# Between two transformer blocks on one core: the low passes of the first projection go ahead of the mean of squares, and half of the third weight slab goes ahead of the gates and decays

## The reference

```python
x = x + rmsnorm(f, norm_mlp_post[l])              # end of the first block
# second block
h = rmsnorm_2(x, norm_mix[layer])                 # x * rsqrt(mean(x*x) + eps) * gain
proj = h @ w_in[layer]
q_nsa, kv_nsa, g_nsa, q_gla, k_gla, v_gla, lr_gla, r_gla, g_merge = split_in_proj(proj)
gates_a = jax.nn.sigmoid(g_nsa)
log_a = jax.nn.log_sigmoid(lr_gla @ gla_gate_w2[layer] + gla_gate_b[layer]) / GLA_GATE_TAU
```

## Time and profile before

| | us |
|---|---|
| median of 3 runs | 1430.52 |
| lowest and highest | 1429.3 and 1430.56 |
| profiled execution, its time | 1429.37 |
| profiled execution, its span | 1427.3 |
| TensorE busy in the span | 1411.2 (99%) |
| VectorE busy in the span | 798.6 (56%) |
| ScalarE busy in the span | 538.3 (38%) |

### The profile page before, as it was taken

How to read it: one execution, slowest core, us unless ns; L and a number is a source line. 1 busy time by engine, 2 the same in 40 slices (tenths; PEclk the granted TensorE clock), 3 DMA queues, 4 the chain that set the end, 5 groups by cost and what they waited for, 6 DMA issues and landing times.

```text
span 1427.3 us, 17634 instructions
## 1 busy us (share of the span) xinstructions
PE 1411.2 (99%) x7303; PEld 1148.1 (80%) x7303; DVE 798.6 (56%) x1126; ACT 538.3 (38%) x768; POOL 173.0 (12%) x145
## 2 busy tenths in 40 slices
PE   7999999999999999999999999999999999999998
PEld 5888788988888888888888776668888888888887
DVE  6998674744234343367494577774545545534533
ACT  6222344643333132255543346662343223212214
POOL 1040013100000000120141612111210000000002
PEclk9999999999999999999999999999999999999999
DMA  6322224112322332323234211112322332232221
GB/s 196 118 89 89 89 89 146 62 59 89 116 90 89 103 104 89 96 89 96 89 81 127 73 60 60 31 31 60 118 89 89 93 113 89 91 116 89 89 89 60
DMA packets 136015, 129.69 MB, mean 91 GB/s; under 512 B 15776, under 2 KB 131424, under 8 KB 135904
## 3 DMA queue, kind: packets, MB, share of 16 engines
q1 hardware_dynamic: 134800, 124.90, 28.1%
q0 software_dynamic: 992, 3.47, 0.8%
q10 hardware_dynamic: 144, 0.20, 0.0%
HBM read 126.06 MB, written 2.10 MB: 90 GB/s over the span
## 4 chain that ended last, share of the span: by engine, by line
PE 95%; ACT 1%; DVE 1%; DMA 1%; issue 1%; POOL 0%; SPq 0%; ACTq 0%
PE gemm L464 75%; PE gemm L572 3%; PE gemm L951 3%; PE misc L972 2%; PE misc L991 1%; PE misc L800 1%; PE gemm L656 1%; PE gemm L603 1%; PE gemm L1032 1%; PE gemm L964 1%; DMA w_raw<-in_w_in 1%; PE misc L964 1%; PE misc L603 1%; PE gemm L1065 1%; PE gemm L677 1%
## 5 line engine op out<-in xcount | busy, mean ns | idle before, releaser
L1668 DVE TENSOR_TENSOR w_lo<-w_raw,w_hi 128x2048 fp32r<-128x2048 f32 (+1 forms) x108 | 245.8, 2276 | 174.7 <-ACT w_hi L1128 174.6
L464 PE MATMUL gemm<-h_hi,w_hi 128*128 128x512 f32 x828 | 325.0, 393 | 0.0
L464 PE MATMUL gemm<-h_hi,w_lo 128*128 128x512 f32 x828 | 322.3, 389 | 0.0
L464 PE MATMUL gemm<-h_lo,w_hi 128*128 128x512 f32 x828 | 322.3, 389 | 0.0
L1128 ACT ACTIVATE w_hi<-w_raw 128x2048 fp32r<-128x2048 f32 (+1 forms) x113 | 213.8, 1892 | 143.9 <-PE gemm L464 139.5
L464 PEld LDWEIGHTS gemm<-h_hi,w_hi 128*128 128x128 f32 x828 | 155.4, 188 | 35.2 <-issue 2.4
L464 PEld LDWEIGHTS gemm<-h_hi,w_lo 128*128 128x128 f32 x828 | 155.5, 188 | 32.4
L464 PEld LDWEIGHTS gemm<-h_lo,w_hi 128*128 128x128 f32 x828 | 155.5, 188 | 32.2 <-issue 0.5
L464 PE MATMUL gemm<-n_hi,w_hi 128*128 128x512 f32 x336 | 130.9, 390 | 0.0
L464 PE MATMUL gemm<-n_lo,w_hi 128*128 128x512 f32 x336 | 130.7, 389 | 0.0
L464 PE MATMUL gemm<-n_hi,w_lo 128*128 128x512 f32 x336 | 130.7, 389 | 0.0
(11 more groups left out here) (463 smaller groups left out, 1967.9 us busy)
## 6 DMA issues: line engine op xcount, KB each, us to landing
w_raw<-in_w_in SPq DMA_DIRECT2D x62, 512.0 KB, 4.6
w_raw<-in_w_down SPq DMA_DIRECT2D x32, 512.0 KB, 4.0
w_raw<-in_w_up SPq DMA_DIRECT2D x28, 512.0 KB, 4.3
w_raw<-in_w_ffn_gate SPq DMA_DIRECT2D x22, 512.0 KB, 4.7
w_raw<-in_w_ffn_up SPq DMA_DIRECT2D x22, 512.0 KB, 4.4
w_raw<-in_w_ffn_down SPq DMA_DIRECT2D x16, 512.0 KB, 4.0
w_raw<-in_w_o SPq DMA_DIRECT2D x8, 512.0 KB, 4.1
w_raw<-in_w_out SPq DMA_DIRECT2D x8, 512.0 KB, 4.0
```

The lines of the kernel that those rows point to most:

```text
L464: mm = nc.tensor.matmul(bank[:], w(s)[:, kt, col0:col0 + P], x(n), start=first, stop=last)
L1668: V.tensor_tensor(part(lo_of(s), s), part(raw_of(s), s), f(part(hi_of(s), s)), SUB).then_inc(S("lo_done"), SLABS_AT[s])
```

## The change

On PE, `first_in` no longer contains the mean nor the spread. Its passes with `u_lo` go tile by tile over the three blocks (one wait for each tile) in place of block by block. Behind it come `mean_rows`, then the first half of the third slab (block m0 + 3) with the spread put in after 5 of its 8 tiles (`SPREAD_AT`), then the gates and decays, then the second half of the third slab (block m0 + 4). On ACT the 8 squares go behind all 8 right half tiles of `u_hi` and behind the high part of the third slab. On DVE the low part of the third slab goes ahead of the reciprocal.

```diff
+    SPREAD_AT = 5
...
             for k in range(KT):
-                pe.wait_ge(S("x1_squared"), KT + k + 1)
-                mm = mean_rows(Y[:, k, :], k == 0, k == KT - 1)
-            mm.then_inc(S("mean_ready"), 1)
-            for n, (s, c0, m) in enumerate(blocks):
-                if n == 1:
-                    spread_rstd(M[2], 4)
-                for k in range(KT):
-                    pe.wait_ge(S("u_lo_ready"), k + 1)
+                pe.wait_ge(S("u_lo_ready"), k + 1)
+                for s, c0, m in blocks:
                     mm = nc.tensor.matmul(G[m % 4][:], hi_of(s)[:, k, c0:c0 + P], ULO[:, k, :], start=False, stop=k == KT - 1)
-                mm.then_inc(S("block_full"), 1)
+                    if k == KT - 1:
+                        mm.then_inc(S("block_full"), 1)
 
         first_in()
+        for k in range(KT):
+            pe.wait_ge(S("x1_squared"), KT + k + 1)
+            mm = mean_rows(Y[:, k, :], k == 0, k == KT - 1)
+        mm.then_inc(S("mean_ready"), 1)
+        pe.wait_ge(S("lo_done"), s0 + 3)
+        gemm(s0 + 2, m0 + 3, range(KT), 0, h(UHI), h(ULO), lambda n: spread_rstd(M[2], 4) if n == SPREAD_AT else None)
         pe.wait_ge(*evac_at(m0))
...
-        slab(s0 + 2, h(UHI), h(ULO))
+        gemm(s0 + 2, m0 + 4, range(KT), P, h(UHI), h(ULO))
         slab(s0 + 3, h(HHI), h(HLO), ready=h_ready(hlo))
...
             nc.scalar.activation(UHI[:, k, SIDE[1]], XT[:, k, SIDE[1]], ACT.Copy, scale=col("norm_mix_2", k)).then_inc(S("u_hi_ready"), 1)
+        split_hi(PH["small"][0] + 2)
+        for k in range(KT):
             nc.scalar.activation(Y[:, k, :], XT[:, k, :], ACT.Square).then_inc(S("x1_squared"), 1)
-        split_hi(PH["small"][0] + 2)
         root_of_rows(5)
...
-        invert_rows(4)
         s0, _, m0, _ = PH["small"]
         split_lo(s0 + 2)
+        invert_rows(4)
```

## The result

| | before | changed |
|---|---|---|
| median of 16 runs, us | 1430.0 | 1436.03 |
| lowest | 1428.7 | 1434.46 |
| profiled execution's span | 1427.3 | 1434.2 |

The changed kernel is slower: ratio 1.0042, 95% interval [1.0029, 1.0054], that is +6.0 us (4.1 to 7.7). The forecast was 1435.2 (1432.9 to 1437.8) and +5.3.

A forecast was written before the change was run, and what follows sets the result against it. TensorE was taken to bound the kernel. Right half -1.6, wait +5.2 and clock +1.7 gave +5.3 us: 1434.7 on the profiled execution, 1435.8 on the median, forecast between at 1435.2, range 1432.9 to 1437.8.

The forecast's parts named there:

- The bound and the room: TensorE bounds; DVE's low part of slab s0 + 3 has 1.82 us of room, and TensorE would wait 5.2 us there.
- The right half: In first_in, u_hi tiles without squares between them come every 0.73 us, at DVE's pace: gain 1.64 us.
- Squares, low passes, mean, spread: Squares and low passes wait for nothing; mean ends 4.1 us late, the copy to rstd comes 5.4 us late.
- The clock: Behind TensorE's stop at slab s0 + 3 the granted clock falls to its lower level: 1.7 us lost, once.
- The next slab: Slab s0 + 4: with the lower clock 5.3 us late without waiting; with full clock waits 0.4, 3.9 late.
- The sum: On the profiled execution, right half, wait and clock: -1.6 + 5.2 + 1.7 = +5.3 us.

The follow-up runs named there:

- run 1: The changed kernel with the spread put in after 2 tiles of block m0 + 3 in place of 5; ratio 1.0019 to the kernel before, median 1433.32 us.
- Run 5: The changed kernel with ACT's squares back between the right half tiles of u_hi; ratio 1.0052 to the kernel before, median 1437.1 us.
- Run 4: The changed kernel with 22 matmuls that nobody reads in front of slab s0 + 3; ratio 1.0034 to the kernel before, median 1435.37 us.
- Run 3: The changed kernel with the high and low parts of slabs s0 + 3 and s0 + 4 moved earlier; ratio 0.9994 to the kernel before, median 1429.99 us.
- Run 3's repetition: The kernel of Run 3 measured once more, unchanged; ratio 1.0 to the kernel before, median 1429.67 against 1429.29 us.
- run 2: The changed kernel with only slab s0 + 3's high and low parts moved earlier; ratio 1.0042 to the kernel before, median 1437.18 us.
- run 9: The kernel before with 8 matmuls that nobody reads behind the third slab; ratio 1.0012 to the kernel before, median 1432.68 us.
- run 10: The kernel before with 16 matmuls that nobody reads behind the third slab; ratio 1.0023 to the kernel before, median 1433.4 us.
- run 6: The kernel before with only ACT's squares moved behind all right half tiles and the third slab's high part; ratio 1.0032, median 1434.08 us.
- run 7: The kernel of Run 3 with 5 wide matmuls between the four groups of narrow ones; ratio 1.0009 to the kernel before, median 1429.93 us.
- run 8: The kernel before with 5 wide matmuls between the four groups of narrow ones; ratio 1.0017 to the kernel before, median 1431.82 us.

## Why the prediction was right, and where it was off

- **The bound and the room.** Right. The room of 1.82 us in front of slab s0 + 3 was the number that mattered; the wait came there, with 5.12 us against 5.2, and run 1 shortened it by 2.05, what the nine matmuls take.
- **The right half.** Right: 0.73 us a tile, and the low passes began 1.5 us sooner, forecast 1.64 (6.38 us from the stage's start, where the mean began at 7.86). Wrong was the sentence that this gain "is lost in the wait, whatever its size". Run 5 took it away and slab s0 + 3 began 1.4 us later, with the wait unchanged. The sum was not touched, since it counted the gain in the times of the mean and of DVE's list. The gain is real; what it can't do is outweigh a spread that stands 5.5 us later.
- **Squares, low passes, mean, spread.** Right in order and, within 0.2 us, in size: the copy to `rstd` was 5.5 us late, forecast 5.4 (5.3 to 5.5). Slab s0 + 3 began 3.8 us late, forecast 3.6.
- **The clock.** Right that it falls, too small in size: I took 1.7 us from the start of the program, the rows show 24.00 - 21.9 = 2.1. Run 4 shows that it is a cost by itself, and what it is worth when slab s0 + 4's own wait comes to light: 1.6. The 1.7 was also read too simply: it is what TensorE's work was drawn out by, but the program lost hardly any of it there, as TensorE had to wait for GpSimd behind that work anyway. Run 3's repetition has no low clock there and comes 0.22 us sooner. Timelines of TensorE, before and in the repetition:

```profile
21.45 3.92 PE L492 MATMUL gemm<-h_hi,w_lo 128*128 128x512 f32 x16 [0.51 <-POOL w_lo L2353]
```

```profile
21.23 3.92 PE L493 MATMUL gemm<-h_hi,w_lo 128*128 128x512 f32 x16 [0.18 <-POOL w_lo L2357]
```

- **When it falls.** The clock fell with 5.12 us of idling (changed), with 3.30 (run 2) and with the 2.48 at the start; it stayed up with 3.07 (run 1). The Trainium skill (TensorE: Matmul & The Clock Gate, HAM oscillation) ties the fall to idle gaps. The 5.12 us, with 0.50 behind them, agree; 2.48 with a fall and 3.07 without show that here a gap's length alone doesn't decide, and behind the narrow matmuls the clock fell without any gap.
- **The next slab.** Right as an order of lateness: with the low clock it didn't wait. Run 2 shows it next in line, and so does run 4: 676.07 to 676.54 is 0.47 us, 0.24 more than a matmul takes, where the forecast with the full clock was a wait of 0.4.
- **The sum.** +5.3 forecast, +5.9 in the stage, +6.0 in the medians. What is missing in the stage is 0.2 of lateness at slab s0 + 3 and 0.4 of clock. That the medians come out as close as they do, and not at the +6.9 of the two profiles, is in part luck: which executions have a low stretch elsewhere differs from one to the next. The profile has +1.6 behind the narrow matmuls, which none of my steps had. It isn't tied to the changed lines: runs 9 and 10, the kernel before with nothing but added matmuls, have it too.

## What to carry to other kernels

Before moving work ahead of a reduction, find what hangs on its result and how much room the first consumer has: here 1.8 us of room stood against a result that came 5.5 us later, and the busy engine gained nothing by having more to do in the meantime. If the order is still wanted, empty the list that hangs on the result first: four moved lines on ACT and DVE turned +5.9 us into -1.5 in the stage. And measure such an edit by its stage in the trace, as a gain of 1.5 us drowns in a median that moves by as much when a later part of the program merely shifts in time.

## What the runs showed that I had not expected

TensorE's granted clock can fall while the engine is never idle. Behind 64 matmuls of 128x31 (3.7 us at full clock) it stayed at 1.00 in one traced execution each of the kernel before, runs 2, 3 and 5 and the repetition of run 3. It was at 0.50 for about 3.4 us in those of the changed kernel and of runs 1, 4 and 9 (some 1.6 us lost), and for about 6.8 us in those of runs 6, 7, 8 and 10 (some 3 us lost; in 7 and 8 with wide matmuls between the narrow ones). The same lines in another kernel, at another time, gave another of the three; why is open. That this also makes the groups in the times of one kernel, as 1428.8 and 1430.4 us of the kernel before, fits their distance, and the mean clocks go the same way (0.998 or 0.999 up to 1429.7 us, 0.997 or 0.998 from about 1430 to 1430.7). It was not shown: only one execution of each run has a trace, and the mean doesn't say where the clock was low.
